# Spare TensorE products behind the sums of five norms

## What is computed

```python
def rms_norm(x, g):
    xf = x.astype(jnp.float32)
    y = xf * lax.rsqrt(jnp.mean(xf * xf, axis=-1, keepdims=True) + RMS_EPS)
    return (y * g.astype(jnp.float32)).astype(x.dtype)

x = x + hybrid_mixer(rms_norm(x, mix_norm_g), w_in, ...)     # norm 1
x = x + conv_glu_ffn(rms_norm(x, ffn_norm_g), w_up, ...)     # norm 2
x = rms_norm(x, final_norm_g)                                # norm 3
h = concatenate([meta_tokens, x])
h = h + mixed(rmsnorm(h, norm1_g_2), ...) @ w_out            # norm 4
h = h + peer_ffn(rmsnorm(h, norm2_g_2), ...)                 # norm 5
out = rmsnorm(h, final_norm_g_2)                             # not touched
```

## Time and profile before

| | us |
|---|---|
| median of 3 runs | 1919.95 |
| these runs | 1916.93 to 1920.94 |
| the profiled execution | 1916.86 |
| its span, first to last instruction | 1915.1 |
| TensorE busy | 1698.7 (89%) |

### The profile page before, as it was taken

The page is one execution under the profiler, slowest core; times in us unless marked ns, Lnnn a source line. Parts: engine busy times, 40 slices in busy tenths (PEclk is TensorE's granted clock), DMA queues, the critical chain, the costliest instruction groups (busy, mean ns, idle before and its releaser), DMA issues. The chain is left out here.

```text
span 1915.1 us, 32548 instructions
## 1 busy us (share of the span) xinstructions
PE 1698.7 (89%) x10946; PEld 1514.3 (79%) x10946; DVE 1213.2 (63%) x2250; ACT 781.5 (41%) x1330; POOL 444.1 (23%) x355
## 2 busy tenths in 40 slices
PE   5988999779995887777495999899999999999997
PEld 5967987669995874554285999899999988888886
DVE  4374214667776352379844599877777467777776
ACT  3441113045552342011232455455555555555554
POOL 0020001214441049206572779500000000000000
PEclk9989999889997898787697999999999999999999
DMA  6412224235552521011143467655555776766663
GB/s 229 154 33 89 77 87 156 66 122 184 183 186 72 200 67 55 22 55 66 44 143 100 133 214 214 199 178 177 176 175 180 231 239 232 242 230 230 236 236 131
DMA packets 93698, 289.40 MB, mean 151 GB/s; under 512 B 11328, under 2 KB 27968, under 8 KB 93248
## 3 DMA queue, kind: packets, MB, share of 16 engines
q1 hardware_dynamic: 93200, 287.61, 45.4%
q10 hardware_dynamic: 432, 0.90, 0.2%
HBM read 270.64 MB, written 17.83 MB: 151 GB/s over the span
## 5 line engine op out<-in xcount | busy, mean ns | idle before, releaser
L257 PE MATMUL bank<-arena_parts 128*128 128x256 f32 (+2 forms) x1664 | 482.2, 290 | 62.2 <-DVE ring_parts L252 23.5
L259 PE MATMUL bank<-arena_parts,ring_parts 128*128 128x256 f32 (+1 forms) x1600 | 454.7, 284 | 0.0
L2297 DVE TENSOR_TENSOR ring_parts<-ring,arena_parts 128x512 fp32r<-128x512 f32 x434 | 293.3, 689 | 131.1 <-ACT arena_parts L2117 104.3
L257 PEld LDWEIGHTS bank<-arena_parts 128*128 128x128 f32 x1664 | 319.7, 192 | 67.2 <-issue 20.1
L258 PE MATMUL bank<-h_parts,arena_parts 128*128 128x256 f32 x1152 | 324.1, 281 | 0.0
L259 PEld LDWEIGHTS bank<-arena_parts,ring_parts 128*128 128x128 f32 x1600 | 307.5, 192 | 0.0
L252 POOL TENSOR_TENSOR ring_parts<-ring,arena_parts 128x1024 fp32r<-128x1024 f32 x79 | 208.6, 2657 | 296.8 <-ACT arena_parts L248 242.9
L258 PEld LDWEIGHTS bank<-h_parts,arena_parts 128*128 128x128 f32 x1152 | 218.1, 189 | 0.0
L228 PE MATMUL bank<-h,ring 128*128 128x256 f32 x896 | 213.8, 398 | 1.0 <-PEq L1203 1.0
L2086 PE MATMUL bank<-arena_parts,x_parts 128*128 128x512 f32 x512 | 202.9, 396 | 2.7 <-DVE x_parts L2324 2.7
L228 PEld LDWEIGHTS bank<-h,ring 128*128 128x128 f32 x896 | 177.8, 202 | 33.1 <-issue 7.8
(11 more groups left out here) (461 smaller groups left out, 3051.4 us busy)
## 6 DMA issues: line engine op xcount, KB each, us to landing
ring<-stream SPq DMA_DIRECT2D x473, 512.0 KB, 3.5
kept<-arena SPq DMA_DIRECT2D x128, 128.0 KB, 2.1
arena<-kept SPq DMA_DIRECT2D x32, 512.0 KB, 4.5
arena<-first SPq DMA_DIRECT2D x1, 2144.0 KB, 8.1
arena<-second SPq DMA_DIRECT2D x1, 1632.0 KB, 7.2
x<-x_t SPq DMA_DIRECT2D x1, 1024.0 KB, 5.8
out<-arena SPq DMA_DIRECT2D x4, 256.0 KB, 2.1
arena<-last ACTq DMA_DIRECT2D x1, 512.0 KB, 3.4
```

What stands on the lines that cost most here:

```text
L257: nc.tensor.matmul(dst, stationary[0], moving[0], start=first, stop=False)
L259: return nc.tensor.matmul(dst, stationary[1], moving[0], start=False, stop=last_one)
L2297: v.tensor_tensor(low[:, s, w], ring[:, s, w], expert_high[:, m % 2, w].bitcast(F32), ALU.subtract)\
```

## The change

`rms_norm` gets a parameter `spare_products`. Behind the four sums TensorE gets so many more products `ones` x `ident` of 128 columns in float32, each into bank 6, which none reads. They wait for nothing and tell nobody. The five norms get 42, 24, 30, 46 and 48 of them, 190 in all.

```diff
--- before.py
+++ after.py
@@ -261,7 +261,7 @@
 
         normed = {"n": 0}
 
-        def rms_norm(src, dst, gain, eps, squares, width=T, beside=None):
+        def rms_norm(src, dst, gain, eps, squares, width=T, beside=None, spare_products=0):
 
 
             n = normed["n"]
@@ -287,6 +287,8 @@
                         mm = nc.tensor.matmul(bank[7][:, 0:width], ones, squares[:, 4 + k, 0:width],
                                               start=k == 0, stop=k == 3)
                     mm.then_inc(total, 1)
+                    for _ in range(spare_products):
+                        nc.tensor.matmul(bank[6][:, 0:P], ones, ident, start=True, stop=True)
 
                 @block.vector
                 def _(dve):
@@ -352,7 +354,7 @@
                 part_high(act, proj_high, n % 8, i + n // 8 + 1)
 
         rms_norm(lambda k: x[:, k, :], lambda k: h[:, k, 0:T], "mix_norm_g", RMS_EPS, squares,
-                 beside=(lambda act: [proj_part_high(act, n) for n in range(AHEAD)], lambda dve: None))
+                 beside=(lambda act: [proj_part_high(act, n) for n in range(AHEAD)], lambda dve: None), spare_products=42)
 
 
         with nc.Block() as block:
@@ -1017,7 +1019,7 @@
                 .then_inc(S("low"), 1)
 
         rms_norm(lambda k: x[:, k, :], lambda k: h[:, k, 0:T], "ffn_norm_g", RMS_EPS, squares,
-                 beside=(lambda act: [ff_high(act, n) for n in (-4, -3)], lambda dve: [ff_low(dve, n) for n in (-4, -3)]))
+                 beside=(lambda act: [ff_high(act, n) for n in (-4, -3)], lambda dve: [ff_low(dve, n) for n in (-4, -3)]), spare_products=24)
         with nc.Block() as block:
             @block.sync
             def _(sp):
@@ -1178,7 +1180,7 @@
                 tiles.advance(FF_LAST, 1, None)
                 for b in range(4):
                     tiles.banks[b] += 1
-        rms_norm(lambda k: x[:, k, :], lambda k: xin[:, k, M:TT], "final_norm_g", RMS_EPS, squares_b := sq2)
+        rms_norm(lambda k: x[:, k, :], lambda k: xin[:, k, M:TT], "final_norm_g", RMS_EPS, squares_b := sq2, spare_products=30)
 
 
         xp = Area(arena_parts[25344])
@@ -1190,7 +1192,7 @@
                 part_high(act, xn_block, n % 4, i + (n // 4 + xn_filled[n % 4]))
 
         rms_norm(lambda k: xin[:, k, :], lambda k: h[:, k, :], "norm1_g_2", RMS_EPS, squares_b, TT,
-                 beside=(lambda act: [xn_part_high(act, n) for n in range(AHEAD)], lambda dve: None))
+                 beside=(lambda act: [xn_part_high(act, n) for n in range(AHEAD)], lambda dve: None), spare_products=46)
         a7 = Area(arena, a6.at)
         us, xm = a7.take(4, TT), a7.take(8, TT)
         zg = a7.take(24, T)
@@ -1909,7 +1911,7 @@
             part_high(act, q_high, QS[m], fillings[m])
 
         rms_norm(lambda k: x[:, k, :], lambda k: h[:, k, 0:T], "norm2_g_2", RMS_EPS, Area(arena).take(KT, T),
-                 beside=(lambda act: [sq_high(act, m) for m in range(AHEAD)], lambda dve: None))
+                 beside=(lambda act: [sq_high(act, m) for m in range(AHEAD)], lambda dve: None), spare_products=48)
         with nc.Block() as block:
             @block.sync
             def _(sp):
```

## The result

| | before | after |
|---|---|---|
| median | 1919.97 us of 6 runs | 1928.58 us of 6 runs |
| these runs | 1916.93 to 1921.92 | 1928.18 to 1930.75 |
| the profiled execution | 1916.86 | 1928.56 |
| its span | 1915.1 | 1926.8 |

The changed kernel takes 1.0049 times the time of the kernel before, with a 95% interval of 1.0036 to 1.0061. It is 8.6 us slower by the medians.

A forecast was written before the change was run, and what follows sets the result against it. TensorE, busy 89% of the span, was taken to bound the kernel, with delays at norm ends passed on whole. 3.6 - 1.6 + 3.1 + 5.4 = +10.5 us, centred on 1918.4, gave 1929, range 1921 to 1936.

The forecast's parts named there:

- TensorE's DRAIN holds the release: At line 270, TensorE's DRAIN ends with the last spare product, last of all engines in norms 1, 3, 4 and 5.
- Price of a product, 0.224 us fast: Each spare product is two records: 0.22 us at the high clock, 0.45 at the low.
- Norm 1, +3.6: 42 products move norm 1's release from 21.1 to 24.7 us, bounds +3.1 and +3.9; restart as slow as before.
- Norm 2, -1.6: 24 products end before the release; ident times x then runs at full clock, saving 1.6 us, bounds -2.6 and +0.8.
- the hole at 414.9: TensorE's 2.92 us wait for VectorE behind norm 2; said to move with TensorE, so that norm 2's gain stays.
- Norms 3 and 4, +3.1: 30 and 46 products: norm 3's release +1.0, norm 4's sums 2.2 us instead of 3.90; together +3.1, bounds +2.2 and +6.0.
- Norm 5, +5.4: 48 products move norm 5's release from 1048.3 to 1053.7 us, bounds +4.5 and +6.1; restart slow again.
- Sum, +10.5: The norms' terms added, 3.6 - 1.6 + 3.1 + 5.4 us, for the whole kernel.
- The rule of the Trainium skill: Avoid long idle gaps between matmul bursts; by it alone the change would gain at every restart. The prediction parted from it.
- The first: Rival: block ends are not late, since the DRAIN does not wait, and all restarts are fast; -10.4, 1908 us, chance 8%.
- The second: Rival: block ends are late, but the clock survives the gaps of 5 to 7 us; +3.4, 1922 us, chance 7%.
- The third: Rival: spare products do not raise the clock and run at 0.45 us each; about 1969 us, chance 3%.

The follow-up runs named there:

- the doubled kernel: 84 spare products behind norm 1's sums and none at the other norms, against the kernel before: 1929.97 beside 1916.76 us, ratio 1.0061.
- the late-but-filled kernel: The changed kernel plus 18, 20 and 26 spare products past the release behind norms 1, 4 and 5: 1920.62 us beside 1916.76 for the kernel before, ratio 1.0021.
- the kernel with products ahead of the sums: Counts 24, 24, 24, 26, 22, with 18, 20, 26 past the release and 4, 8, 4, 8, 8 ahead of the sums: ratio 0.9951 to the kernel before.

## Why the prediction was right

The forecast was 1929, the measured median 1928.58, the direction slower. The mechanism is right: the block's end waits for TensorE. That the number is met to half a microsecond is partly luck, as the sum's own point below shows. Point by point:

- **TensorE's DRAIN holds the release.** Right, in all four norms named: the DRAIN of TensorE ends last, with the last spare product, 0.2 us ahead of the release. In norm 3 by little: its block is 0.1 longer, where +1.0 was reckoned.
- **Price of a product, 0.224 us fast.** Right: 9.68 us for 42, where only the first two records start 0.21 us apart and the rest 0.11; 10.1 us for the second 42 of the doubled kernel, with a later rise of the clock in it.
- **Norm 1, +3.6.** Measured +3.2. The clock rose earlier than I took (the records begin at 14.4 us, at 1.00). Restart slow, right, but not "as slow as before": 6.0 us at 0.50 instead of 3.4, which costs 1.3 us by the sum's own rule of one half, outside my bounds of 0 and -2.2. Faster stretches later in the mixers hid it.
- **Norm 2, -1.6.** The mechanism is right: `ident` times `x` took 3.67 us, 3.6 was said. That it stays was wrong for the profiled execution: the step that failed is "the hole at 414.9 moves with it, as said, so it stays". The hole moved, but the clock around it was low twice as long (6.8 us instead of 3.4), and of 1.6 us 0.5 was left. In other kernels the hole left the clock alone, and the part was up to 3.1 us shorter.
- **Norms 3 and 4, +3.1.** Measured +3.7, from two terms that were mis-sized: norm 3's +1.0 was 0.1, and norm 4's sums took 3.31 us instead of 2.2, since the clock fell in the midst of them. That an idle time of 2.3 us leaves it alone, as I took it from the 2.74 in the earlier trace rows, held in one execution (2.10 us for the same sums in the kernel with norms 3 and 4 alone) and not in this. In two more with the same idle time of 2.32 us it did not hold either: 3.19 us for these sums in the late-but-filled kernel, and the restart behind norm 2 in the kernel with products ahead of the sums. The kernel before had a warning close by. Its sums of norm 5 follow 2.92 us of idle time and took 2.93 us, and the clock falls in their midst:

```profile
1038.90:1039.70 0.80, 0.80 (x4) 0.72 (x5) 0.80 (x3) 0.80 (x2) 0.00 (x0) 1.00 0.03 10
1039.90:1041.70 1.80, 1.80 (x5) 1.00 (x3) 0.00 (x0) 1.78 (x3) 0.00 (x0) 0.50 0.00 0
```

- **Norm 5, +5.4.** Measured +5.1 in the changed kernel and in the one with norm 5 alone.
- **Sum, +10.5.** In the profile 11.7, between medians 8.6. The 1929 rested on a middle of 1918.4 for the kernel before; its median over six runs is 1919.97, so that centre was 1.6 too low and the sum 1.9 too high for the medians. The two errors cancel, which is luck.
- **The rule of the Trainium skill** ("TensorE: Matmul & The Clock Gate", section "Why this matters for your kernels"), to keep idle gaps out between bursts: the kernel with products on both sides of the release follows it, and the trace agrees (clock 1.00 at the restarts behind norms 1, 2, 4 and 5, ratio 0.9951). The changed kernel lost at the ends of its blocks, 12.1 us in the five norms together.
- **The rivals.** The first fell: no release came while products ran. The second fell too: at 5.00, 5.71 and 7.05 us of idle time the clock was low at the restart. It was made true by hand in the late-but-filled kernel: +3.9 us, where +3.4 had been reckoned. The third fell with the lengths of the runs (9.68 us for 84 records, where 18.9 had been reckoned at the low clock). Its +1.5 at norm 2 is not what its own price gives: 391.77 + 10.8 + 0.2 is 402.8, 4.5 behind 398.3, and its time would be 1972 instead of 1969. That changes neither the range nor the chances.

Not settled is what decides whether an idle time of 2.3 to 3.0 us costs the high clock. The same stretches of the program showed both. So the saving at a restart or a hole can be named only as a range, while the cost of a late release came out nearly as reckoned (+3.2 and +5.1 us for norms 1 and 5, where +3.6 and +5.4 had been said).

## What to carry to other kernels

Work that fills an engine's idle time is free only up to the next point at which others wait for that engine. Before adding it, look for such a point (a block's end, a barrier, a DRAIN) inside the idle time, and count the slack up to there, here 6.3 us of 11.3. Then fill both sides of it separately, starting the run in time that is free: behind 6.6 us of idle time 18 products took 6.28 us here instead of 4.26, and held up the real work.

## What was not expected of the hardware

TensorE's holes of nearly the same length had different consequences for its clock: 2.91 us with the clock at 1.00 throughout, 2.92 with 3.4 us at 0.50, which begin 0.8 us behind the hole's end, and 2.96 with 6.8 us at 0.50, which begin 1.1 us ahead of it. Even 2.32 us led to a restart at 0.50 in one kernel (5.32 us for `ident` times `x`). Unchanged pieces of the program, the last 870 us above all, differ by up to 4 us between profiled executions (866.8 to 870.7), with the low-clock stretches in them. A change worth 2 us can't be told from a single pair of profiles in this kernel.
